# Attention's first units between the query projections, with the compressed branch behind them

## The reference, cut to what matters

```python
proj = xn @ w_in                       # queries (16 heads of 64) and gates
q = rmsnorm(proj[..., :1024].reshape(B, T, G, HP, dh), q_norm_g) * dh ** -0.5
# compressed branch: 15 blocks of 32 tokens, stride 16
flat = (blocks + pos).reshape(B, -1, Hk, CMP_BLOCK * dh)
k_cmp = rmsnorm(gelu(flat_k @ w1_k) @ w2_k, k_norm_g[0]); v_cmp = gelu(flat_v @ w1_v) @ w2_v
# for each of three branches (compressed, selected, window):
l = einsum(q, k) + rel_bias[bucket(distance)]
o += gate * (masked_softmax(l) @ v)
```

## Time and profile before

| what | us |
|---|---|
| runs of the kernel before | 1446.25, 1439.06, 2052.23 |
| their median | 1446.25 |
| the profiled execution | 1440.81 |
| its span, first to last instruction | 1439.2 |
| PE busy | 1380.9 (96%) |
| DVE busy | 433.9 (30%) |
| ACT busy | 307.4 (21%) |
| POOL busy | 144.5 (10%) |

### The profile page before, as it was taken

How to read it: one execution, slowest core, us unless ns; L and a number is a source line. 1 busy time by engine, 2 the same in 40 slices (tenths; PEclk the granted TensorE clock), 3 DMA queues, 4 the chain that set the end, 5 groups by cost and what they waited for, 6 DMA issues and landing times.

```text
span 1439.2 us, 36218 instructions
## 1 busy us (share of the span) xinstructions
PE 1380.9 (96%) x16208; PEld 831.3 (58%) x16208; DVE 433.9 (30%) x646; ACT 307.4 (21%) x495; POOL 144.5 (10%) x215
## 2 busy tenths in 40 slices
PE   7999999999997799999999999999999999999995
PEld 7999999998895583343343343343343343344343
DVE  5985555555567730110110110110110110110120
ACT  5744543434545821000000000000000000000000
POOL 0600100001203705001001001001001001001001
PEclk9999999999997998999999999999999999999998
DMA  9853465557986056999999999999999999999993
GB/s 280 261 168 118 152 202 176 177 189 166 215 242 240 1 206 252 402 418 402 419 418 400 419 418 401 419 418 402 418 418 401 418 419 402 419 418 390 419 399 143
DMA packets 132786, 454.83 MB, mean 316 GB/s; under 512 B 12452, under 2 KB 74109, under 8 KB 132643
## 3 DMA queue, kind: packets, MB, share of 16 engines
q1 hardware_dynamic: 126386, 435.11, 78.0%
q0 software_dynamic: 6080, 17.37, 5.2%
q10 hardware_dynamic: 176, 0.14, 0.0%
HBM read 436.46 MB, written 14.55 MB: 313 GB/s over the span
## 4 chain that ended last, share of the span: by engine, by line
PE 86%; DMA 8%; DVE 3%; ACT 2%; issue 1%; POOL 0%; SPq 0%; POOLq 0%; ACTq 0%; DVEq 0%
PE ps L1647 85%; DMA more<-in_moe_w_gu 4%; DMA ring<-in_moe_w_down 3%; ACT x_hi L926 1%; DMA ring<-in_a_w_in 1%; DVE arena L1492 1%; DVE arena L1489 1%; DMA arena<-item_rows,arena 0%; ACT arena L1134 0%; PE ps L1951 0%; ACT x_hi L956 0%; DVE arena L1493 0%; ACT between L1155 0%; POOL arena L788 0%; PE ps L1759 0%
## 5 line engine op out<-in xcount | busy, mean ns | idle before, releaser
L1647 PE MATMUL ps<-more,arena 128*32 128x448 f32 x3456 | 330.0, 539 | 4.7 <-DMA more<-in_moe_w_gu 4.7
L1616 DVE TENSOR_TENSOR arena<-arena,ps 128x448 f32<-128x448 f32 x48 | 29.8, 621 | 769.6 <-PE ps L1647 765.4
L1647 PE MATMUL ps<-ring,arena 128*32 128x448 f32 x2688 | 258.7, 542 | 1.2 <-ACT arena L1201 1.2
L1647 PEld LDWEIGHTS ps<-more,arena 128*32 128x32 f32 x3456 | 105.1, 110 | 225.4 <-issue 212.1
L1647 PE MATMUL ps<-ring,between 128*32 128x256 f32 x3360 | 189.6, 379 | 0.5 <-DMA ring<-in_moe_w_down 0.4
L1647 PEld LDWEIGHTS ps<-ring,arena 128*32 128x32 f32 x2688 | 82.2, 110 | 168.3 <-issue 158.2
L522 DVE TENSOR_TENSOR w_lo<-ring,w_hi 128x2048 fp32r<-128x2048 f32 x67 | 153.5, 2294 | 77.8 <-ACT w_hi L516 77.7
L1647 PEld LDWEIGHTS ps<-ring,between 128*32 128x32 f32 x3360 | 105.2, 110 | 86.9 <-issue 7.8
L516 ACT ACTIVATE w_hi<-ring 128x2048 fp32r<-128x2048 f32 x67 | 127.6, 1910 | 97.5 <-PE ps L1647 87.9
L1647 PE MATMUL ps<-more,between 128*32 128x256 f32 x2016 | 115.3, 379 | 0.0
L1212 ACT ACTIVATE arena<-ps 128x448 f32<-128x448 f32 x48 | 26.1, 543 | 414.2 <-PE ps L1647 414.2
(11 more groups left out here) (269 smaller groups left out, 1137.0 us busy)
## 6 DMA issues: line engine op xcount, KB each, us to landing
more<-in_moe_w_gu SPq DMA_DIRECT2D x144, 896.0 KB, 20.0
ring<-in_moe_w_gu SPq DMA_DIRECT2D x112, 896.0 KB, 19.5
ring<-in_moe_w_down SPq DMA_DIRECT2D x80, 896.0 KB, 20.0
more<-in_moe_w_down SPq DMA_DIRECT2D x48, 896.0 KB, 20.2
ring<-in_ffn_w_gu SPq DMA_DIRECT2D x22, 1024.0 KB, 5.1
ring<-in_a_w_in SPq DMA_DIRECT2D x16, 1024.0 KB, 11.6
ring<-in_ffn_w_down SPq DMA_DIRECT2D x11, 1024.0 KB, 5.0
ring<-in_w_kv SPq DMA_DIRECT2D x6, 1024.0 KB, 4.9
```

Source lines behind the costliest of these rows:

```text
L1616: dve.tensor_tensor(SU[:, a, :], SU[:, a, :], ps[:, b, 0:QUARTER], ALU.mult).then_inc(bank_free[b], 1)
L1647: return pe.matmul(o, w, x, start=start, stop=stop, **kw)
```

## The change

It does the following.

- The bias rows are written 16 times to DRAM instead of 128 times, and read back in eight DMAs of 16 partitions each, each from the same 16 rows.
- TensorE's order becomes: query jobs 0 and 1, sum 0, job 2, sum 1, scores of units 0 and 1, job 3, sum 2, scores of units 2 and 3, sum 3, block products, loop from s = 4. Norm work on ScalarE and VectorE is interleaved to match; parts 2 and 3 stand behind units 1 and 2.
- The block products of keys and values are one job: stationary is the block input (60 columns), moving are 256 columns of w1, keys in output partitions 0 to 59 and values in 64 to 123. The gelu is applied to this, the result is transposed (124 columns, two transposes), and ScalarE spreads it. These steps stand at s = 4 (gelu, with both table switches), 6 (transposes, spread), 7 (keys), 8 (key sum, `VCZ`) and 9 (`KCZ`). `CMP_AT` becomes s = 10 and 18.
- The compressed values are added behind the units of an output bank, four products in a row (`block_values`), with s = 16, 20, 28 and 36; the first product of a unit pair clears the bank.
- The three `mixB` splits stand behind units 3, 5 and 17 (`SPLIT_AT`).
- Query jobs get banks 2 and 3, sums 5 and 6, block products 7, transposes 6. Small arrays of maxima and sums move to places of their own.

```diff
+COPIES = 16
...
-        job(("qB", b))
+        job(("qB", b), 2 + b % 2)
...
-        job(("qsum", b))
-    for s in range(2):
-        job(("hid", s), 2 + s)
+        job(("qsum", b), 5 + b % 2)
+    job(("hid",), 7)
+    job(("hidT",), 6)
...
-        CMP_AT = [2 + HB // 2 * ORDER.index(tt) for tt in range(TT)]
+        CMP_AT = [10 + HB // 2 * ORDER.index(tt) for tt in range(TT)]
+        SPLIT_AT = (3, 5, 17)
...
-                           biasrow[:, 0:row].unsqueeze(1).to_broadcast([HB, P, row])).then_inc(rows_out, 16)
+                           biasrow[:, 0:row].unsqueeze(1).to_broadcast([HB, COPIES, row])).then_inc(rows_out, 16)
             add_squares(2)
             pool.wait_ge(rows_out, 16)
-            pool.dma_start(BD, bass.AP(scratch, P - 1, [[HB * row - 1, P], [row, HB], [1, T]])).then_inc(bias_in, 16)
+            for p in range(0, P, COPIES):
+                pool.dma_start(BD[p:p + COPIES, :, :], bass.AP(scratch, P - 1 - p, [[HB * row - 1, COPIES], [row, HB], [1, T]])).then_inc(bias_in, 16)
...
+            def blocks_gelu():
+                act.preload_act_table_set("gelu_apprx_tanh_and_others")
...
+                act.activation(GB[0:G * NCMP], ps[0:G * NCMP, k, 0:HID], ACT.Gelu_apprx_tanh).then_inc(gelu_done, 1)
+                act.activation(GB[64:BOTH], ps[64:BOTH, k, 0:HID], ACT.Gelu_apprx_tanh).then_inc(bank_free[k], 1)
+                act.preload_act_table_set("natural_log_exp_and_others")
...
+            query_squares(0)
+            refill(make_hi, act, ("qB", 0))
+            query_squares(1)
+            query_factors(0)
+            query_squares(2)
+            query_factors(1)
             for s in range(len(units) + LAG):
...
+                if s == 1:
+                    query_squares(3)
+                    query_factors(2)
+                if s == 2:
+                    query_factors(3)
+                if s == 4:
+                    blocks_gelu()
+                if s == 6:
+                    blocks_spread()
+                if s == 7:
+                    block_keys()
+                if s == 8:
...
+                if s in SPLIT_AT:
+                    refill(make_hi, act, ("qB", 1 + SPLIT_AT.index(s)))
...
+            query_scaled(1)
+            query_normed(0)
+            query_scaled(2)
+            query_normed(1)
...
-            for n in range(3):
-                refill(make_lo, dve, ("qB", n + 1))
-                biased(n)
...
-                if 2 < s < len(units):
+                if s < len(units):
                     biased(s)
+                if s == 1:
+                    query_scaled(3)
+                if s == 2:
+                    query_normed(3)
...
+                if s == 1:
+                    query_normed(2)
+                if s - 1 in SPLIT_AT:
+                    refill(make_lo, dve, ("qB", 1 + SPLIT_AT.index(s - 1)))
...
-            dense("qB")
-            for n in range(4):
+            def query_sum(n):
...
+            project(("qB", 0), True)
+            project(("qB", 1), False)
+            query_sum(0)
+            project(("qB", 2), False)
+            query_sum(1)
+            pe.wait_ge(keys_copied, 16 * 4)
+            scores(0)
+            project(("qB", 3), False)
+            query_sum(2)
+            scores(2)
+            query_sum(3)
+            pe.wait_ge(rc_ready, 2 * G)
+            b = free_bank(pe, ("hid",))
+            for half in range(2):
+                w = [raw_arrived(pe, ("w1", 2 * s + half)).rearrange("p (k n) -> p k n", n=HID) for s in range(2)]
+                for k in range(CMP // 4):
+                    for s in range(2):
+                        last = mm(ps[64 * s:64 * s + G * NCMP, b, 0:HID], RC[:, s, CMP // 4 * half + k, :], w[s][:, k, :],
+                                  half == 0 and k == 0, half == 1 and k == CMP // 4 - 1, skip_group_check=True)
+                last.then_inc(w1_used if half == 0 else bank_full[b], 1)
...
-            for s in range(0, len(units) + LAG + 2, 2):
-                if 0 < s < len(units):
+            for s in range(4, len(units) + LAG + 2, 2):
+                if s < len(units):
                     scores(s)
+                if s == 6:
+                    blocks_turned()
...
+                if s == 6:
+                    block_keys()
+                if s == 8:
+                    block_key_sum()
                 if s > LAG:
                     values(s - LAG - 2)
+                for n in range(2 * TT):
+                    if s == max(8 * n + 6 + LAG + 2, CMP_AT[units[8 * n][0]] + 6):
+                        block_values(n)
```

More of the change, by code:

```diff
@@ L1095, in _, with query_squares @@
             last.then_inc(bank_free[k], 1)
-            for b in range(4):
+            def query_squares(b):
                 evacuated(act, ("qB", b))
@@ new lines, in blocks_spread @@
+            def blocks_spread():
+                k = filled(act, ("hidT",))
+                turned_hid = ps[:, k, 0:2 * P].rearrange("p (m n) -> p m n", m=2)
+                act.activation(GH[:, :, :], turned_hid[:, :, 0:G * NCMP], ACT.Copy).then_inc(gelu_done, 1)
+                for m in range(2):
+                    blocks = turned_hid[:, m, 64:BOTH].rearrange("p (g n) -> p g n", g=G)
+                    last = act.activation(GHV[:, m, :].rearrange("p (g h n) -> p g h n", g=G, h=HP),
+                                          blocks.unsqueeze(2).to_broadcast([P, G, HP, NCMP]), ACT.Copy)
+                last.then_inc(bank_free[k], 1)
@@ L1456, in query_scaled, with query_normed @@
                 dve.tensor_tensor(QT[:, 2 * b:2 * b + 2, :], by_token(k), per_token, ALU.mult).then_inc(bank_free[k], 1)
+            def query_normed(b):
+                dve.wait_ge(rs_b, b + 3)
+                evacuated(dve, ("qB", b))
+                v = slice(2 * b, 2 * b + 2)
+                dve.scalar_tensor_tensor(QT[:, v, :], QT[:, v, :], cols[:, ROW_Q:ROW_Q + 1], qsq[:, v, :], ALU.mult, ALU.mult).then_inc(norm_b, 1)
             query_scaled(0)
             refill(make_lo, dve, ("qB", 0))
+            dve.wait_ge(shifted, 16 * 8)
             for s in range(2):
-                dve.wait_ge(shifted, 16 * 8)
                 for g in range(G):
@@ L2001, in _, with block_values @@
-            last.then_inc(bank_full[b], 1)
-            pe.wait_ge(sq_b, 3)
-            b = free_bank(pe, ("kcsum",))
-            mm(ps[:, b, 0:G * NCMP], halves, kcsq, True, True).then_inc(bank_full[b], 1)
+                                last.then_inc(pv_done, 1)
+            def block_values(n):
+                tt, first = units[8 * n]
+                b = J[("OT", n)][0]
+                evacuated(pe, ("PCT", tt))
+                evacuated(pe, ("vc",))
+                for j in range(4):
+                    last = mm(ps[:, b, P * j:P * j + P], VCZ[:, first // 2 + j, :], PCT[:, tt, first // 8, :], False, True, skip_group_check=True)
+                last.then_inc(bank_full[b], 1)
@@ new lines, in blocks_turned, with block_keys @@
+            def blocks_turned():
+                evacuated(pe, ("hid",))
+                pe.wait_ge(gelu_done, 1)
+                b = free_bank(pe, ("hidT",))
+                for m in range(2):
+                    last = pe.transpose(ps[:, b, P * m:P * m + BOTH], GB[0:BOTH, P * m:P * m + P], ident[0:BOTH, 0:BOTH])
+                last.then_inc(bank_full[b], 1)
+            def block_keys():
+                pe.wait_ge(gelu_done, 2)
+                b = free_bank(pe, ("kc",))
+                for m in range(2):
+                    last = mm(ps[:, b, 0:G * NCMP], w2[:, 0, m, :, :].rearrange("p a d -> p (a d)"), GH[:, m, :], m == 0, m == 1)
+                last.then_inc(bank_full[b], 1)
+                evacuated(pe, ("hidT",))
+                b = free_bank(pe, ("vc",))
+                for a in range(2):
+                    for m in range(2):
+                        last = mm(ps[0:ROWS_C, b, DH * a:DH * a + DH], GHV[:, m, ROWS_C * a:ROWS_C * a + ROWS_C], w2[:, 1, m, 0, :], m == 0, m == 1)
+                last.then_inc(bank_full[b], 1)
```

107 lines of the change are left out of this document (33 added, 74 removed).

## The result

The changed kernel takes 1446.58 us (median of 9 runs, 1444.77 to 1794.95), the kernel before 1442.89 us (9 runs, 1439.06 to 2052.23). The ratio is 1.0032, with a 95% interval of 1.0019 to 1.0044: some 4.6 us slower, where I had forecast 2 us faster. (The ratio is not the quotient of the medians, which lie 3.7 us apart.) The longest run of each kernel is a disturbed one and is not in the ratio. Each run also lists its mean granted clock of TensorE, the share of full speed that it was allowed: 0.974 to 0.978 in the eight other runs of the changed kernel, 0.979 to 0.985 in the 29 runs of the kernel before that stood beside the second group of experiments. The two ranges do not meet.

The account below looks back on a forecast made before the run. VectorE was taken to pace attention's units, and the expert layer only to shift. -2.1 + 0.8 = -1.3 us at half clock, -4.7 at full; -2 was taken, predicting a 1441 us median, range 1427 to 1453.

Parts of the forecast that it names:

- Part 1: Bias rows written 16 instead of 128 times, eight reads landing between 373 and 382: cost and gain 0.
- Part 2: Projections and first units: first scores at 412.7, block products 7 us, loop from 429.5, some 19 us ahead at unit 4.
- Rival (b): Block products' column groups don't share the array: 14.4 us, price 5.5 us, result 1446.5 us; chance 0.10.
- the table price of the Trainium skill: ScalarE table switch with drain about 2.7 us, not 1.28: two switches cost 2.8 us more, time 1444.
- Rival (c): ScalarE's queue holds block chain back; half clock until unit 16, 2 us per step pair, about 1444; chance 0.15.
- Part 3: Units carry splits and compressed work: unit 9 at 454.4, unit 16 at 471.1, last weight at 498.2, gain 2.1 us.
- The gelu gap: TensorE waits for the gelus from 432.7 to 436.6; at half clock five later steps cost 3.4 us more.
- From unit 16 to the end it was 22.75: Last units on VectorE: 22.75 plus compressed tile 3.1 and split 2.3, less 1.0 for filled waits, ending at 498.2.
- Part 4: Tail: four compressed value products behind the last units, 1.2 us less 0.4 saved, so 0.8 us later.
- My mechanism for the front half: Units start before the projections end, so unit 16 begins at 471.1 against 477.58.

Follow-up runs that it names:

- run 8: Kernel before with only the bias edit (16 copies written, eight reads of 16 partitions): 1442.86 us, ratio 1.0001.
- run 5: Changed kernel with its third weight split behind unit 21 instead of 17, after the second tile's compressed weights: 1443.07 us, ratio 1.0003.
- run 4: Changed kernel with seven unread products added in TensorE's gap ahead of the second tile's compressed transposes: 1442.54 us, ratio 0.9998.
- run 6: Changed kernel with block products in pairs ahead of the unit's values, plus seven unread products before the second tile's compressed transposes: 1439.07 us, ratio 0.9974.
- Run 3: Changed kernel with compressed value products ahead of the unit's values, in pieces of two and two to six units earlier: 1442.52 us, ratio 0.9993.
- run 9: Changed kernel with unread extra products in TensorE's idle stretches around the first tile's block products: 1439.12 us, ratio 0.9983.
- run 12: Kernel before with five unread products in each of TensorE's two gaps around its first compressed tile: 1444.7 us, ratio 1.0012.

## Why the prediction was wrong

**Part 1 was right in its price, 0.** The DMA view of the changed kernel (KB each, us from issue to landing):

```profile
arena<-bias_rows POOLq DMA_DIRECT2D x8, 256.0 KB, 11.3
bias_rows<-arena POOLq DMA_DIRECT2D x1, 384.0 KB, 5.7
```
```profile
359.65 4.45 POOL L765 DMA_DIRECT2D arena<-bias_rows  x8
```

The write took 5.7 us instead of 36.6, and the reads were issued in 4.45 us (I had 5), from 359.65 on. The 11.3 us to land are a median. The first read lands 5.1 us behind its issue, the eighth, issued at 363.5, after 18.5 us, and the others between them, 2.0 to 3.6 us apart: the reads came one behind the other, and the bias stood at 382.0, not in the middle of my 373 to 382 but at its end. From the first issue that is 22.4 us, near the 24.4 that I had as the upper bound and above the 15.5 of the one big read. Nothing waited for it, and run 8 measures the edit alone as nothing.

**Part 2 was right**, to about 1 us once the late first mark (1.4 us) is taken off. TensorE, and ScalarE's table switches:

```profile
413.69 1.13 PE L1692 MATMUL ps<-arena 64*128 64x512 f32 x4 [0.94 <-issue]
...
423.68 7.12 PE L1692 MATMUL ps<-ring,arena 128*60 128x256 f32 x64
430.73 1.13 PE L1692 MATMUL ps<-arena 64*128 64x512 f32 x4
...
437.11 0.43 PE L2059 MATMUL ps<-const,xn 124*128 124x124 f32 x2 [3.16 <-ACT xn L1124]
```
```profile
434.98 1.28 ACT L1120 ACT_TABLE_LOAD   x1
436.27 0.38 ACT L1123 ACTIVATE xn<-ps 60x256 f32<-60x256 f32 x1
436.67 0.38 ACT L1124 ACTIVATE xn<-ps 60x256 f32<-60x256 f32 x1
437.07 1.28 ACT L1125 ACT_TABLE_LOAD   x1
438.37 0.60 ACT L1190 ACTIVATE between<-ps 128x512 f32<-128x512 f32 x1
```

First scores at 413.69 less 1.4 (412.7 forecast), block products 7.12 us (7), the loop from 430.73 less 1.4 (429.5). Rival (b) is out: the two column groups shared the array at 0.11 us a record. So is the table price of the Trainium skill (ScalarE: Activation LUTs, "What ACT_TABLE_LOAD costs"): the instruction behind each load starts 0.01 and 0.02 us after it, with no drain between them, and a switch costs 1.28 us here, not some 2.7. (Rival (c) added 2 times 2 us to 1441 and wrote 1444; it is 1445.)

**Part 3 was right up to unit 16.** The gelu gap came (3.16 us), the clock fell from 438 on as I had assumed, unit 8's scores ran at half clock, and units 9 and 16 began at 454.3 and 470.69, less 1.4 at 452.9 and 469.3, where I had 454.4 and 471.1. Rival (c), half clock until unit 16, did not come; it was half clock at 458 to 462 only.

**The step that failed is "From unit 16 to the end it was 22.75. Added are the other compressed tile, 3.1, and the third split, 2.3; I take off 1.0".** It ends in 27.2 us; measured it was 34.1 (504.76 - 470.69). Three things are wrong in it:

- Its base was short by 1.0. 500.33 is the weight write of unit 30; unit 31's is at 501.37, so the stretch was 23.8. I had taken the last row before a wait of 0.68 us for the end.
- It adds VectorE's work and takes the waits for TensorE to shrink by 1.0. They grew by 5.4: from 0.61, 1.00 and 0.24 (1.85 in all) to 0.66, 1.81, 0.69, 3.18 and 0.91 (7.25). I did note that VectorE "now has this work to fill the waits". But the split is not only work for VectorE. It stands between the compressed scores and the weights that TensorE waits for, so what fills VectorE's time empties TensorE's. That made the gap of 3.53 us (1.39 with the split elsewhere, run 5).
- I had weighed the clock for 438 to 454 alone, since the earlier trace rows show it there. I did not ask whether the change makes another such gap. It does, and at 1.2 GHz the value and block products behind it take 4.06 us instead of 2.25 (1.98 + 2.08 against 1.09 + 1.16 in run 4). Behind them VectorE waits 3.18 us for the next scores; with full clock, in run 4, it doesn't. Runs 4 and 6 give 2.6 and 4.3 us of the stretch back without moving the split.

With full clock and the block products out of the way (run 6) the stretch is 29.6 us by reciprocals; my sum on the corrected base, 23.6 + 3.1 + 2.3 - 1.0, is 28.0. The added work was sized right to 1.6 us, about the one wait for TensorE (1.66 us, ahead of unit 18) that run 6 still has. The half clock, the block products' place and the stalls that came with them are the rest of the 33.9.

**Part 4 was mis-sized.** 0.8 us was forecast for the tail and 3.5 measured. The four block products are only a part of it: the clock falls once more, at 506, after two windows in which TensorE was busy for 0.74 and 1.24 us of 2, and the values (1.98), the block products (2.08) and the first two sweeps of the output projection (3.02 and 2.57 instead of 1.98 and 2.08) run slowly. Run 3 takes the block products out of the tail and has 45.2, as before; run 9 keeps them and has 45.5 at full clock. So the clock is nearly all of it. Why it fell is not settled: in run 9 TensorE was as thinly busy there (0.85 and 1.12 us of 2, in 500 to 504), and the clock stayed up.

**The signs.** None of my rivals was this one. (b) gave the measured number, 1446.5, for a reason that did not occur; it must not be counted as a hit. My mechanism for the front half was right and its gain was even larger than forecast (8.3 us instead of 6.5 to unit 16), and it was given back by a mechanism which I had seen in the trace and priced in one place only.

## What to carry to other kernels

When a step moves between a producer and what TensorE waits for, price it twice: as work on its own engine, and as a gap on TensorE, with what stands behind the gap at half clock for a while (here 482 to 489 us). Look at the granted clock in windows of the stretch, not in the mean: 0.974 against 0.984 was a true hint, but part of it came from stretches that the change doesn't touch, and in run 12 a higher mean bought nothing. A few products that nobody reads are a cheap test of such a theory, since they change nothing but the gap; whether they also pay has to be measured each time, since in the kernel before the same filling raised the clock and won nothing.

## What the runs showed of the hardware that I had not expected

- The same gap can cost more or less. With 3.53 us of idle TensorE ahead of the same transposes, the clock was at or below 0.73 until 490 in the changed kernel, and back at 1.00 from 486 in run 9, whose schedule is 0.6 us earlier. The tail had half clock for 10 us in the one and none in the other. A shift of well under a microsecond in front thus went with several behind it, which no sum over durations foresees. Each is one trace; the median of run 9 is 7.5 us below that of the changed kernel.
- Two products in different column groups, float32, 60 weight columns and 256 moving ones, run side by side: 64 records in 7.12 us, 0.11 each, half of what one record takes by its columns (0.225, worked out in the prediction from the earlier trace rows). The trace shows how: the starts come in pairs, 0.007 us apart, and a new pair every 0.216 us.
- Seven float32 products of 256 columns without dependence take 3.29 us for 14 records, 0.235 each (0.216 from start to start), close to that figure.
- Eight DMAs of 256 KB, each into 16 partitions, issued within 4.45 us from one queue, landed one behind the other over 22.4 us; one DMA of the same 2048 KB into 128 partitions took 15.5 us. No run separates the number of DMAs from the partitions that each one reaches, and other transfers shared the time.
